# Second layer's first mixer: weight slots in another order, the attention chains begun between them, and the first slot behind the experts loaded while the last expert units run

## The reference

```python
def even_mixer(hn, w_in, q_gain, k_gain, ret_gain, w_out):
    p = hn @ w_in                                   # 1024 -> 3584
    sb_q, sb_k, sb_v, r_q, r_k, r_v, r_g = jnp.split(p, cuts, axis=-1)   # 512 each
    qa = rms_norm(to_heads(sb_q, 8), q_gain)
    ka = rms_norm(to_heads(sb_k, 8), k_gain)
    out_a = from_heads(stick_breaking_attention(qa, ka, to_heads(sb_v, 8)))
    qb, kb = rope(to_heads(r_q, 4), pos), rope(to_heads(r_k, 4), pos)
    ret = retention_chunkwise(qb, kb, to_heads(r_v, 4), log_gamma)
    out_b = from_heads(rms_norm(ret, ret_gain)) * jax.nn.silu(r_g)
    return jnp.concatenate([out_a, out_b], axis=-1) @ w_out
```

## Time and profile before

| | |
|---|---|
| median of 3 runs | 1822.02 us (1819.06 to 1826.24) |
| the profiled execution, its own time | 1819.95 us |
| its span in the profile | 1818.1 us |
| mean granted clock of PE | 0.976 |
| busy: PE, DVE, ACT, POOL | 94%, 68%, 52%, 20% of the span |

### The profile page before, as it was taken

One profiled execution on the slowest core, in us unless ns is written; L12 is line 12 of the kernel. 1 busy time (PEld: TensorE's weight loads), 2 busy tenths in 40 slices (PEclk: granted clock), 3 DMA queues, 4 the chain that ended last, 5 costly groups with the idle time before them and its releaser, 6 DMA issues.

```text
span 1818.1 us, 30514 instructions
## 1 busy us (share of the span) xinstructions
PE 1706.2 (94%) x12046; PEld 1582.2 (87%) x12046; DVE 1243.6 (68%) x1916; ACT 936.7 (52%) x1155; POOL 364.0 (20%) x417
## 2 busy tenths in 40 slices
PE   7996989999999999999999998987999987999999
PEld 6996988999999999988888887977999776789987
DVE  4665547898998666666666666576788454568873
ACT  5463554545555555545445455664555356345552
POOL 0000000000657777210000000000355000004530
PEclk9998999999999999999999999998999999999999
DMA  7432423577555555777777775522555542335553
GB/s 281 163 116 82 151 93 120 175 233 235 187 174 193 185 192 186 266 234 238 237 238 238 235 228 206 183 83 85 184 186 184 179 148 99 110 118 184 186 185 116
DMA packets 73503, 323.50 MB, mean 178 GB/s; under 512 B 8615, under 2 KB 8871, under 8 KB 55312
## 3 DMA queue, kind: packets, MB, share of 16 engines
q1 hardware_dynamic: 58576, 285.38, 46.1%
q0 software_dynamic: 5568, 19.38, 3.6%
q10 hardware_dynamic: 9216, 16.78, 2.5%
HBM read 303.68 MB, written 17.83 MB: 177 GB/s over the span
## 4 chain that ended last, share of the span: by engine, by line
PE 64%; DVE 14%; issue 8%; POOL 7%; ACT 5%; DMA 1%; SPq 0%; DVEq 0%; POOLq 0%; ACTq 0%
PE bank L563 8%; PE bank L565 7%; PE bank L564 7%; PE bank L902 7%; PE bank L904 6%; PE bank L903 6%; POOL upad L494 5%; PE bank L858 5%; PE bank L862 5%; PE bank L861 5%; DVE wlo L1656 3%; PE bank L870 3%; DVE lo_u L1991 2%; POOL fs L498 2%; ACT whi L1195 1%
## 5 line engine op out<-in xcount | busy, mean ns | idle before, releaser
L1383 ACT ACTIVATE hi_u<-raw_u 128x1024 fp32r<-128x1024 f32 x256 | 272.0, 1063 | 287.2 <-PE bank L902 169.7
L1656 DVE TENSOR_TENSOR wlo<-raw,whi 128x2048 fp32r<-128x2048 f32 x139 | 318.6, 2292 | 130.3 <-PE bank L563 112.7
L1195 ACT ACTIVATE whi<-raw 128x2048 fp32r<-128x2048 f32 x139 | 266.7, 1918 | 122.4 <-PE bank L563 116.5
L1991 DVE TENSOR_TENSOR lo_u<-raw_u,hi_u 128x1024 fp32r<-128x1024 f32 x192 | 238.2, 1241 | 86.7 <-PE bank L858 75.3
L858 PE MATMUL bank<-xh,hi_u 128*128 128x256 f32 x1024 | 291.9, 285 | 3.8 <-DVE lo_u L1991 3.6
L861 PE MATMUL bank<-xl,hi_u 128*128 128x256 f32 x1024 | 285.6, 279 | 0.0
L862 PE MATMUL bank<-xh,lo_u 128*128 128x256 f32 x1024 | 285.4, 279 | 0.0
L563 PE MATMUL bank<-nh,whi 128*128 128x256 f32 x904 | 256.8, 284 | 4.7 <-DVE wlo L1656 2.6
L565 PE MATMUL bank<-nh,wlo 128*128 128x256 f32 x904 | 252.9, 280 | 0.0
L564 PE MATMUL bank<-nl,whi 128*128 128x256 f32 x904 | 252.9, 280 | 0.0
L458 POOL TENSOR_SCALAR oh<-kept,sel_T 128x128 f32<-128x128 f32 x256 | 198.1, 790 | 266.6 <-ACT sel_T L1415 179.3
(11 more groups left out here) (394 smaller groups left out, 3568.4 us busy)
## 6 DMA issues: line engine op xcount, KB each, us to landing
raw<-in_weights SPq DMA_DIRECT2D x139, 1024.0 KB, 4.8
raw_u<-in_experts SPq DMA_DIRECT2D x256, 512.0 KB, 4.0
aside<-a_out ACTq DMA_DIRECT2D x64, 256.0 KB, 3.1
a_in<-aside POOLq DMA_DIRECT2D x64, 256.0 KB, 3.7
const<-in_const SPq DMA_DIRECT2D x1, 1409.0 KB, 9.5
const<-in_const POOLq DMA_DIRECT2D x1, 1409.0 KB, 6.3
h<-in_x SPq DMA_DIRECT2D x1, 1024.0 KB, 4.8
memx<-in_mem SPq DMA_DIRECT2D x1, 1024.0 KB, 11.5
```

Of the source, the lines that this page charges most:

```text
L1195: a(A(whi[:, n % HIGH, :], raw[:, n % RAW, :], ACT.Copy), S("weights_hi"))
L1383: a(A(hi_u[:, u % HIGH_U, :], raw_u[:, u % RAW_U, :], ACT.Copy), S("unit_high"))
L1656: v(V.tensor_tensor(wlo[:, n % LOW, :], raw[:, n % RAW, :], whi[:, n % HIGH, :].bitcast(F32), ALU.subtract), S("weights_split"))
L1991: v(V.tensor_tensor(low_unit(u), raw_u[:, u % RAW_U, :], hi_u[:, u % HIGH_U, :].bitcast(F32), ALU.subtract), S("unit_split"))
```

## The change

It has these parts.

1. SP loads slot 38 before the last four expert units, no longer behind them; ACT and DVE split it between the last units.
2. At the end of the expert layer DVE adds all four pieces of the result before it does norm 4's low parts; PE does c0 after all four norm transposes, not a quarter between them. The splits of slots 39, 40, 41 and 42 are set between the steps of the final norm (`final_squares`, `final_means`, `block1_done`).
3. The columns of `w_in` are reordered on the host: the stick-breaking values (`ev2`) come last, as c12 and c13; retention's q and k are c4 to c7, its values c8, c9, its gates c10, c11.
4. The chains begin earlier between the slots: `head_norms` behind c5 (was c7), `stick_scores(0)` behind c6 (was c8), `suffix_sums(0)`, `retT` and `stick_scores(1)` behind c9, `rscore`, `suffix_sums(1)` and `rout` behind c11. Only `sbout` and `rT` are left behind c13.
5. `rotary` works on q or k for both token blocks, six instructions of 512 elements for each (were 24 of 256 in all). The decayed scores have a tile of their own, `rW`. Retention's norm squares run on ACT, its gain is multiplied into the gates ahead, and the rest is eight `scalar_tensor_tensor` that read PSUM.
6. `res2`'s first product takes its chunks in the order 0, 1, 4, 5, 6, 7, 2, 3, and waits for each part of its input where it needs it.

```diff
+         + [("norm4", 4), ("even", 6), ("sbT", 4), ("even", 1), ("sbz0", 4), ("even", 3), ("sbR0", 4), ("retT", 4), ("sbz1", 4),
+            ("even", 2), ("rscore", 4), ("sbR1", 4), ("rout", 4), ("even", 2), ("sbout", 1), ("rT", 2), ("sbout", 1)]
...
             for u in range(UNITS):
+                if u == UNITS - 4:
+
+                    for i in range(2):
+                        sp.wait_ge(S(f"aside{i}"), 16 * (PAIRS // 2))
+                    sp.wait_ge(S("unit_used"), P + 2)
+                    weights(BEFORE)
...
+            for i in range(14):
+                if i:
+                    chunk("even", i, "even", i, normed[4])
+                if i == 5:
+                    head_norms()
+                elif i == 6:
+                    stick_scores(0)
+                elif i == 9:
+                    suffix_sums(0)
+                    retention_heads()
+                    stick_scores(1)
+                elif i == 11:
+                    retention_scores()
+                    suffix_sums(1)
+                    retention_values()
+            stick_values(0)
             pe.wait_ge(S("ret_out"), 1)
             for tb in range(TB):
                 bank = open_("rT", tb)
                 for c in range(4):
                     mm = pe.transpose(bank[:, c * P:(c + 1) * P], sq4[:, tb, c * P:(c + 1) * P], ident)
                 close(mm)
+            stick_values(1)
...
+            def softplus(grp, n):
+                for c in range(4):
+                    bank = full(f"sbz{grp}", c)
+                    a(A(sbA[:, c, :], bank[:, 0:384], ACT.Abs))
+                a(A(sbA[:, :, :], sbA[:, :, :], ACT.Exp, scale=-1.0))
+                even(n)
+                a(A(sbA[:, :, :], sbA[:, :, :], ACT.Ln, bias=1.0), S("sb_log"))
...
+            softplus(0, 9)
+            even_out(7)
+            even(10)
+            even_out(8)
+            even(11)
+            even_out(9)
+            stick_exp(0)
+            for k in range(4):
+                bank = full("retT", k)
+                dst = (rqT, rkT)[k % 2][:, :, (k // 2) * P:(k // 2 + 1) * P]
+                drain(A(dst, bank[:, :].rearrange("p (c t) -> p c t", c=4), ACT.Copy), "retT", k)
+            softplus(1, 12)
...
+            even(8)
+            even(9)
+            stick_logs(0)
+            even(10)
+            rotary(1)
+            stick_exponents(0)
+            even(11)
+            stick_weights(0)
+            even(12)
+            stick_logs(1)
```

More of the change, by code:

```diff
@@ L940, in _ @@
                 norm_T(4, h, i)
-            for i in range(1, 4):
+            w = slot("even", 0)
+            bank = open_("even", 0)
+            for i in range(4):
                 mm = rows_of(4, i, bank, outs_N(bank), w, normed[4])
-            cur["b"] = of_even
             close(mm)
@@ new lines, in retention_values @@
+            def retention_values():
+                drained("even", 8, 9)
+                for hd in range(4):
+                    drained("rscore", hd)
+                    bank = open_("rout", hd)
+                    for tb in range(TB):
+                        out = bank[:, tb * P:(tb + 1) * P]
+                        mm = pe.matmul(out, rW[:, hd, tb * P:(tb + 1) * P], ev[5][:, 0, hd * P:(hd + 1) * P],
+                                       start=True, stop=(tb == 0))
+                        if tb == 1:
+                            mm = pe.matmul(out, rW[:, hd, T:T + P], ev[5][:, 1, hd * P:(hd + 1) * P], start=False, stop=True)
+                    close(mm)
@@ new lines, in _ @@
+            even_out(0)
+            even_out(1)
+            even(5)
+            even_out(2)
+            even_out(3)
+            even(6)
+            act.wait_ge(S("sb_means"), 1)
+            a(A(small[:, 256:288], small[:, 256:288], ACT.Sqrt), S("sb_roots"))
+            even_out(4)
+            even(7)
+            even_out(5)
+            for k in range(4):
+                bank = full("sbT", k)
+                dst = (sbqT, sbkT)[k % 2][:, :, (k // 2) * P:(k // 2 + 1) * P]
+                drain(A(dst, bank[:, :].rearrange("p (c t) -> p c t", c=4), ACT.Copy, scale=small[:, 240 + k % 2:241 + k % 2]),
+                      "sbT", k)
@@ L2140, in _, with even, head_squares_of @@
-            stick_exponents(1)
+            def even(n):
+                split_lo(BEFORE + n)
+            def head_squares_of(q):
+                drained("even", 2 * q, 2 * q + 1)
+                for tb in range(TB):
+                    x, y, at = halves(q, tb)
+                    v(V.tensor_tensor(y, x, x, ALU.mult))
+                    v(V.tensor_reduce(small[:, at:at + 8], y, AX, ALU.add))
+            even(4)
+            head_squares_of(0)
+            even(5)
+            head_squares_of(1)
@@ L2168, in _ @@
[L2168 to L2169 removed]
+            for hd in range(4):
+                for tb in range(TB):
+                    at = 288 + 2 * hd + tb
+                    ins = V.scalar_tensor_tensor(out=sq4[:, tb, hd * P:(hd + 1) * P], in0=turn("rout", hd)[0][:, tb * P:(tb + 1) * P],
+                                                 scalar=small[:, at:at + 1], in1=ev[6][:, tb, hd * P:(hd + 1) * P],
+                                                 op0=ALU.mult, op1=ALU.mult)
+                    if tb == 0:
+                        v(ins)
+                drain(ins, "rout", hd)
```

271 lines of the change are left out of this document (113 added, 158 removed).

## The result

The changed kernel takes 1796.22 us in the median of 4 runs (1794.36 to 1798.86), the kernel before 1824.13 us in 4 (1819.06 to 1826.35): a ratio of 0.9852, with a 95% interval of 0.9825 to 0.9879. The profiled execution took 1796.64 us. The page of its profile begins as follows.

What follows compares the result with a forecast made beforehand. PE, busy 94% of the span, was taken as the bound, leaving holes and half-clock work to win. `res2` 23.8 us earlier plus 1.2 of clock takes 25.0 off 1819.95; adding 2.1 for the median gives 1797 us, range 1791 to 1801.

Steps and rivals of the forecast that it cites:

- Before the mixer: Last expert units: early load of slot 38 loses 0 us; its low split delays the last unit 0.75 us, regained at once.
- c0 to c9: First mixer slots on PE: c1 starts at 1118.9, the holes of 3.80 and 1.85 go, no hole over 0.5 from c1.
- The chain on ACT and DVE: Softplus, rotation, exponents and drains: rotation ends at 1177.9, first `retT` drain at 1183.7, second group's logarithms at 1200.2.
- A: PE's hole before `retT`, waiting for DVE's rotation: 1.4 us.
- B: PE's hole before c10, waiting for ACT's drain of `retT`: 2.4 us.
- C: PE's hole before the second suffix sums, waiting for DVE's `stick_logs`: 2.2 us.
- The clock by the length of the hole: PE's clock fell behind a hole of 2.44, not 1.85; a fall behind B or C loses 1.7 us; 1.0 allowed.
- The rule on table loads: ACT's table switches: 2.66 us each by the skill, giving some 1802 us; rejected for the trace's 1.28 us load.
- Tighter chains: Rival, 20%: splits and drains on ACT fall behind one another, holes A, B and C total 12 to 20 us; 1801 to 1812.
- PE's floor: Rival, 8%: shorter instructions cover the holes, `res2` starts 3 us after the no-hole time of 1214.6; 1788 to 1791 us.
- taken back: Rival, 5%: feed-forward behind `res2` starts with fewer slots ahead, slots 52 to 55 wait, 17 us; 1814 to 1822 us.
- wait behind chain steps: Rival, 3%: slots 44 to 51 find both splits queued behind chain steps, 34 us lost against 25 gained; 1831 us.

Runs made afterwards that it cites:

- splits behind the norm: Changed kernel with the splits of slots 39, 40 and 41 put back behind the steps of the final norm; 1804.07 us.
- the two runs on the kernel before: Kernel before the change with splits moved early between the final norm's steps: those of slots 39 and 40, 1824.44 us; those of 39 to 42, 1819.07 us.
- both splits off the chain: Changed kernel with the splits of slots 48 (DVE) and 50 (ACT and DVE) moved behind the chain steps they preceded; 1793.29 us.
- split 48 off: Changed kernel with DVE's low split of slot 48 behind the first group's exponents, no longer before the rotation; 1797.0 us.
- changed kernel again: Changed kernel once more without an edit, on the chip of the next three runs; 1796.01 us.
- The best version: Changed kernel with the splits of slots 48 and 50 off the chain and ACT draining `retT` ahead of the first group's Exp; 1789.6 us.
- narrow rotation: Changed kernel with the rotation in twelve instructions of 256 elements for each of q and k, not six of 512; 1800.12 us.

## Why the prediction was right, point by point

The forecast was 1797 us, and 1796.22 were measured; of the stage I had 23.8 off and 25.3 came off. That the two times agree to 0.8 us is in part luck: I had 25.0 off, the medians differ by 27.9 and the two profiled executions by 23.3, and the median of before moved by 2.1 with a fourth run. By its own steps:

- **Before the mixer.** The hole of about 1 us before the last unit is there, 1.05. The nil for the load that goes ahead of four units held as well: with slot 38 behind the units the stage is the same.
- **c0 to c9.** Right: no hole, and c1 at 1120.91, which is 1119.2 when the later mark is taken off (I had 1118.9). The run with the splits behind the norm shows that the holes go because of the splits' place, the two runs on the kernel before that it isn't enough to bring the first two ahead.
- **Rotation and exponents on DVE.** Six instructions of 0.69 with 0.03 between them, and the exponents in 2.33: my estimates held.
- **The chain on ACT and DVE.** Less the 1.7 of later mark, the rotation ended at 1177.95 (I had 1177.9), the drain of `retT` 0 at 1183.86 (1183.7), and the last mask before the second suffix sums at 1200.39 (1200.2). This is the mechanism of the forecast, and it held to 0.2 us.
- **The three holes.** Their places and releasers were right, their sizes not: A 2.08 (1.4), B 0.80 (2.4), C 2.73 (2.2), 5.6 together where I had 6.0. All three lie outside the bounds that I gave as a sign (1 to 2, 2 to 3, 0.5 to 2.5). A hole is the difference between that chain and PE, and it was PE's side that was off. It reached A 0.6 us earlier (the first suffix sums end at 1177.63, 1175.9 less the mark, for 1176.5), and the clock failed as a term: I asked whether it would fall behind B or C and allowed 1.0; it fell behind A, at a cost of 1.6 to 1.7 in `retT` and `sbz1`, and that filled B. When it spared A, in the second profile of the same kernel, B was 2.42.
- **The clock by the length of the hole.** I read from 2.44 and 1.85 that longer holes cost clock. That reading was wrong: it fell behind holes of 2.08 (changed kernel), 2.39 (both splits off the chain) and 2.73 (split 48 off), and not behind 2.07 (changed kernel again), 2.39 (split 48 off), 2.43 and 2.53 (splits behind the norm) or 2.73 (changed kernel). Below 2.07 none is seen to bring a fall.
- **Slots.** I used 5.65 us. c0 to c5 take 33.17, 5.53 each, which over fourteen slots is 1.7 us less. That is more than the difference between 104.5 and 105.7 in PE's work, so my small groups were a little too short.
- **Retention's norm.** It ended at 1218.79, or 1217.1 less the mark, 2.2 us ahead of its need; I had 1216.5. Moved behind c13, with `rscore` and `rout`, it costs 5.6 us of waiting again.
- **The start of `res2`.** At 1223.48, against my 1223.3; but with 1.7 us of later mark in it. Counted from the mark it is 1.5 us earlier than I had. That is my two last terms, 1.0 for the clock and 0.5 for hand-offs: both fell before the end of a wait for ACT or DVE, so they cost next to nothing. The faster slots are no reason up to C, where PE waits anyway; from the start of the second suffix sums on PE took 21.3, for my 21.6.
- **The rule on table loads.** The Trainium skill ("ScalarE: Activation LUTs", section "What ACT_TABLE_LOAD costs") would have added about 1380 ns of drain to each switch, and have given 1802. This trace disagrees: 1182.15 + 1.28 = 1183.43, and Exp starts at 1183.45; 1193.05 + 1.28 = 1194.33, and Ln at 1194.35. Nor is there idle time ahead of the load: the split before the second ends at 1191.11 + 1.92 = 1193.03.
- **The rivals.** Tighter chains (holes of 12 to 20 us) did not come: 5.6. PE's floor was not reached either. The best version, with 1.8 us of holes behind c0, comes near it, at 1789.6 where that rival, meant for the changed kernel itself, had 1788 to 1791. Nothing was taken back behind `res2`: 571.2 against 571.0. The slots did not wait behind chain steps.

Two of my later expectations, each for one split taken off the chain, counted on the time that the split takes. In one the clock took it back behind C, in the other PE's own work became the limit 0.4 us on.

## What to carry to other kernels

Write out, for each engine, what stands ahead of the instruction that PE waits for: here two weight splits and four drains stood on the chain for no reason of data, and moving all of them shortened the stage by 5.0 us, where moving either split alone won nothing. Move a whole run of splits together: bringing two of four ahead of a norm only moved the hole to a later slot. And count from a mark that no version moves, as the start of the stage varied from 1098.2 to 1102.9 between these profiles, more than most single edits changed.

## What the runs showed of the hardware

- **The clock falls behind a hole or it doesn't, for the same program.** The granted clock was 0.57 behind hole A of 2.08 us in one execution (`retT` 3.27 us) and 1.00 behind A of 2.07 in another (1.97). By the lengths of the same groups of matmuls with and without a fall, one behind a hole of 2.1 to 2.7 cost 1.4 to 1.7 us of PE's work. Behind longer holes the cost varied: 1.6 and 1.8 behind 3.71 (retention behind c13) and 3.80 (the kernel before), but 2.6 behind 3.25 (narrow rotation) and 2.7 behind 3.40 (splits behind the norm). Where PE came to a wait for another engine soon after, a fall cost nothing of the time: the stage is 123.55 with the fall behind A and 123.72 with it behind B. In all profiles of the changed order it fell behind one or two of the three holes, and behind none in the one profile of the best version, whose largest hole behind c0 was 1.27. What decides was not settled.
- **Equal slots have more than one rate at a granted clock of 1.00.** c0 to c5 took 33.17 us in the changed kernel and 34.23 in the best version; c7 to c9 took 16.45 in both; c12 and c13 took 11.07 in both, and 11.48 with split 48 off the chain. The matmuls are the same. The cause is open, and it is as large as a small edit's effect.
- **A hole marked "issue" was a wait for another engine.** Before, the holes ahead of the suffix sums were put to "issue"; in the first profile of the changed kernel, the one at 1202.19 is put to DVE's mask (`sbL`, L1850), and PE starts 0.10 behind its end. In the second profile of the same kernel the hole at 1204.79 is put to "issue", though the same mask ends 0.10 before it there too (1204.00 + 0.69 = 1204.69), as it does before the 2.44 of the kernel before.
